# Transformer block on one core: key picking, projections and attention units woven in another order

## The reference, cut to what matters

```python
p = rms_norm(x, mix_norm[l]) @ w_in[l]
pa, pb, pc = split_cols(p, GROUP_SPLITS)
ya = dsa_attention(pa, ...)     # 8 heads; each query sees at most 128 picked keys
yb, v_first = rwkv7_time_mix(pb, ...)   # recurrence, 4 heads
yc = gated_deltanet(pc, ...)            # recurrence, 4 heads
x = x + concatenate([ya, yb, yc], -1) @ w_out[l]

# dsa_attention, for each block i of 128 queries:
score = einsum(relu(logits of 8 index heads), wib)      # 128 queries x 512 keys
_, idx = lax.top_k(score, 128)                          # n_sel = min(256, 512 // 4)
p = softmax(q . k over the picked keys);  o = p @ v
```

## Time and profile before

| | us |
|---|---|
| median of 3 runs (4070.52 to 4078.71) | 4076.85 |
| profiled execution | 4068.68 |
| its span | 4066.7 |
| PE busy | 3803.9 (94%) |
| DVE busy | 1396.7 (34%) |
| ACT busy | 1407.5 (35%) |
| POOL busy | 1339.4 (33%) |
| granted TensorE clock, mean | 0.931 |

### The profile page before, as it was taken

One profiled execution on the slowest core, in us unless ns is written; L12 is line 12 of the kernel. 1 busy time (PEld: TensorE's weight loads), 2 busy tenths in 40 slices (PEclk: granted clock), 3 DMA queues, 4 the chain that ended last, 5 costly groups with the idle time before them and its releaser, 6 DMA issues.

```text
span 4066.7 us, 54295 instructions
## 1 busy us (share of the span) xinstructions
PE 3803.9 (94%) x23012; PEld 3130.1 (77%) x23012; DVE 1396.7 (34%) x2950; ACT 1407.5 (35%) x2395; POOL 1339.4 (33%) x639
## 2 busy tenths in 40 slices
PE   8987999998799979999989789999999999879999
PEld 7876888887588868888757678888888866768887
DVE  2345111334521132113774741112112574662111
ACT  2453222335422233223543432223223454433222
POOL 3103444420244444444210124444444420104443
PEclk9988999998799989999976889999999995889999
DMA  4101333320133333333200023333333310003332
GB/s 118 47 16 58 93 99 96 89 63 11 47 88 98 97 92 100 100 95 95 58 20 2 2 64 98 104 96 102 96 102 93 83 52 1 2 23 88 93 99 93
DMA packets 406785, 292.37 MB, mean 72 GB/s; under 512 B 18032, under 2 KB 356880, under 8 KB 406544
## 3 DMA queue, kind: packets, MB, share of 16 engines
q1 hardware_dynamic: 400976, 284.69, 23.6%
q10 hardware_dynamic: 5136, 2.96, 0.3%
q0 software_dynamic: 432, 1.25, 0.1%
HBM read 286.77 MB, written 2.10 MB: 71 GB/s over the span
## 4 chain that ended last, share of the span: by engine, by line
PE 54%; DVE 6%; ACT 2%; issue 1%; POOL 0%; ACTq 0%; DVEq 0%
PE ps L705 9%; PE ps L706 9%; PE ps L707 9%; PE ps L766 6%; PE ps L769 6%; PE ps L768 6%; PE ps L1285 2%; PE ps L820 2%; PE ps L837 1%; PE ps L1074 1%; PE ps L828 1%; PE ps L688 1%; PE ps L1245 0%; POOL wl L2861 0%; ACT wh L2291 0%
## 5 line engine op out<-in xcount | busy, mean ns | idle before, releaser
L2861 POOL TENSOR_TENSOR wl<-wraw,wh 128x1024 fp32r<-128x1024 f32 (+2 forms) x532 | 1246.3, 2343 | 2258.5 <-ACT wh L2291 2258.5
L705 PE MATMUL ps<-x_T,wh 128*128 128x512 f32 (+1 forms) x2672 | 1028.2, 385 | 18.9 <-POOL wl L2861 9.8
L706 PE MATMUL ps<-x_T,wh 128*128 128x512 f32 (+1 forms) x2672 | 1021.1, 382 | 0.0
L707 PE MATMUL ps<-x_T,wl 128*128 128x512 f32 (+1 forms) x2672 | 1020.7, 382 | 0.0
L2291 ACT ACTIVATE wh<-wraw 128x1024 fp32r<-128x1024 f32 (+2 forms) x532 | 548.8, 1032 | 1104.0 <-PE ps L769 595.0
L705 PEld LDWEIGHTS ps<-x_T,wh 128*128 128x128 f32 x2672 | 510.4, 191 | 130.9 <-issue 30.0
L707 PEld LDWEIGHTS ps<-x_T,wl 128*128 128x128 f32 x2672 | 510.1, 191 | 95.6
L706 PEld LDWEIGHTS ps<-x_T,wh 128*128 128x128 f32 x2672 | 510.5, 191 | 93.5 <-issue 0.5
L766 PE MATMUL ps<-wh,h_T 128*128 128x512 f32 x1056 | 411.3, 390 | 0.0
L769 PE MATMUL ps<-wh,h_T 128*128 128x512 f32 x1056 | 410.9, 389 | 0.0
L768 PE MATMUL ps<-wl,h_T 128*128 128x512 f32 x1056 | 410.8, 389 | 0.0
(11 more groups left out here) (716 smaller groups left out, 4861.4 us busy)
## 6 DMA issues: line engine op xcount, KB each, us to landing
wraw<-in_ffn_w_gate_dram SPq DMA_DIRECT2D x88, 512.0 KB, 3.8
wraw<-in_ffn_w_up_dram SPq DMA_DIRECT2D x88, 512.0 KB, 3.8
wraw<-in_w_in_dram SPq DMA_DIRECT2D x82, 512.0 KB, 3.8
wraw<-in_ffn_w_down_dram SPq DMA_DIRECT2D x80, 512.0 KB, 3.7
wraw<-in_w_gate_dram SPq DMA_DIRECT2D x44, 512.0 KB, 3.8
wraw<-in_w_up_dram SPq DMA_DIRECT2D x44, 512.0 KB, 3.8
wraw<-in_w_down_dram SPq DMA_DIRECT2D x40, 512.0 KB, 3.7
wraw<-in_w_o_dram SPq DMA_DIRECT2D x16, 512.0 KB, 3.7
```

Source lines behind the costliest of these rows:

```text
L705: mm(b[:, t0:t1], wh[:, k, :], xTh[:, k, t0:t1], k == 0, False)
L706: mm(b[:, t0:t1], wh[:, k, :], xTl[:, k, t0:t1], False, False)
L707: ins = mm(b[:, t0:t1], wl[:, k, :], xTh[:, k, t0:t1], False, k == 7)
L2861: tt(wl, raw_of(w), wh.bitcast(F32), ALU.subtract).then_inc(*g.sig("w", "lo", w))
```

## The change

The order of blocks in picking, in their index sums and in the attention units becomes 3, 2, 1 (after block 0 for the units), as `PICKS`. One picking step is made in every round. A column projection's 24 matmuls are split into three pieces of 9, 9 and 6, one in each round (three in a warm-up round), and its bank is held from its first piece to the second piece of the next projection. Its evacuation comes in the round after its last piece. While units of block 3 and 2 are open, units start in even rounds only, and in every round for block 1. `gates` advances in every third round while projections last.

Counted out, the numbered rounds after are: block 0's units start in n = 0, 2, ..., 14; block 3's in n = 18, 20, ..., 32; block 2's in 36, 38, ..., 50; block 1's in every round from 52 to 59. Picking runs for block 3 in n = 1 to 16, block 2 in 18 to 33, block 1 in 35 to 50. Pieces run in n = 0 to 26, the last evacuation in n = 27. The recurrence starts in n = 32, the last unit's last step is in n = 62, and tile 0 has its 32nd step, the last of its solving, in n = 63.

```diff
@@ -291,19 +291,23 @@
         yield
 
 
+PICKS = (3, 2, 1)
+SUMS = [(i, h) for i in PICKS for h in range(8)]
+
+
 def index_lane(skew, summed, work):
 
     for t in range(26):
         if 0 <= t - skew < 24:
-            work(1 + (t - skew) // 8, (t - skew) % 8)
+            work(*SUMS[t - skew])
         if t in (9, 17, 25):
-            summed.add(1 + (t - 9) // 8)
+            summed.add(PICKS[(t - 9) // 8])
         yield
 
 
 def top_lane(summed, masks, first, work, last):
 
-    for i in (1, 2, 3):
+    for i in PICKS:
         while i not in summed:
             yield
         first(i)
@@ -318,11 +322,14 @@
 COLS2 = (6, 0, 1) + tuple(range(7, 13)) + (2, 3, 4, 5)
 
 
-def project_lane(skew, work):
-
-    for t in range(14):
-        if 0 <= t - skew < 13:
-            work(COLS2[t - skew])
+def project_lane(piece, work):
+
+
+    for t in range(40):
+        if t % 3 == 0 and t:
+            work(COLS2[t // 3 - 1])
+        if t < 39:
+            piece(COLS2[t // 3], t % 3)
         yield
 
 
@@ -330,13 +337,15 @@
 
 
 
+
     while next(heads, "end") != "end":
-        next(project)
+        for _ in range(3):
+            next(project)
         next(gates)
         for _ in range(2):
             next(index)
     masks.add(0)
-    todo = [(h, i) for i in range(4) for h in range(8)]
+    todo = [(h, i) for i in (0,) + PICKS for h in range(8)]
     live, n, clear = [], 0, []
     chain = tile_rounds(tiles, clear)
     while todo or live or top:
@@ -349,17 +358,16 @@
         for g in list(live):
             if next(g, "end") == "end":
                 live.remove(g)
-        if todo and (n % 2 == 0 or not project) and todo[0][1] in masks:
+        if todo and (n % 2 == 0 or todo[0][1] == PICKS[-1]) and todo[0][1] in masks:
             live.append(unit(*todo.pop(0)))
             next(live[-1])
         next(index, None)
-        for _ in range(2 if project else 1):
-            if top and next(top, "end") == "end":
-                top = None
-        if project and n % 2 == 0:
+        if top and next(top, "end") == "end":
+            top = None
+        if project:
             if next(project, "end") == "end":
                 project = None
-            else:
+            elif n % 3 == 0:
                 next(gates)
         n += 1
     over()
@@ -584,7 +592,7 @@
         for h in range(4):
             UNITS1 += [("stick", h, 0)] + [("mla", h, i) for i in range(4)]
         UNITS1 += [("swa", h, i) for h in range(4) for i in range(4)]
-        UNITS3 = [("dsa", h, i) for i in range(4) for h in range(8)]
+        UNITS3 = [("dsa", h, i) for i in (0,) + PICKS for h in range(8)]
         GROUP = {"fox": 0, "mla": 1, "stick": 2, "swa": 3}
 
         place = {}
@@ -715,6 +723,29 @@
                     pe.wait_ge(*at(*ready))
                 pe.wait_ge(*at("w", "lo", w))
                 cols_F(w, b, 0, T).then_inc(*pe.sig("w", "used", w))
+
+            def piece_F(_, n):
+
+                if n == 0:
+                    w = use()
+                    _, free = bank(("F", w), ("ev", w), hold=True)
+                    pe.wait_ge(*free)
+                    pe.wait_ge(*at("w", "lo", w))
+                w = wat[0] - 1
+                i = book.bank[("F", w)]
+                if n == 1:
+                    held.discard(book.bank.get(("F", w - 1)))
+                wh, wl = hl_of(w)
+                for k in ((0, 1, 2), (3, 4, 5), (6, 7))[n]:
+                    mm(psum[i][:, :], wh[:, k, :], xTh[:, k, :], k == 0, False)
+                    mm(psum[i][:, :], wh[:, k, :], xTl[:, k, :], False, False)
+                    ins = mm(psum[i][:, :], wl[:, k, :], xTh[:, k, :], False, k == 7)
+                if n == 2:
+                    ins.then_inc(*pe.sig("w", "used", w))
+
+            def last_F(k):
+                if k == COLS2[-1]:
+                    held.discard(book.bank[("F", wat[0] - 1)])
 
             def first_F(name, src, ready, done=()):
 
@@ -1426,7 +1457,7 @@
                 mixer_rounds(heads(l), lambda h, i: unit3(l, ("dsa", h, i)),
                              index_lane(0, summed, lambda i, h: index_sum(l, i, h)),
                              top_lane(summed, masks, nothing, nothing, nothing),
-                             project_lane(0, lambda k: proj_F()), gates(l),
+                             project_lane(piece_F, last_F), gates(l),
                              [rec_tile(l, j, stock) for j in range(4)], masks, over)
                 barrier("o", l)
                 to_T(("out", l), mx, lambda j, c: ("bar", "o", l, "dve"))
@@ -1891,7 +1922,7 @@
 
             def index_sum(l, i, h):
                 acc = msk[:, i - 1, 0:(i + 1) * P]
-                rb = scr[5 + (8 * i + h) % 3]
+                rb = scr[5 + SUMS.index((i, h)) % 3]
                 v.wait_ge(*at("pk", "relu", l, i, h))
                 if h == 0:
                     ins = ts(acc, rb[:, 0:(i + 1) * P], wiv[:, i, h:h + 1], None, ALU.mult)
@@ -2234,7 +2265,7 @@
                 mixer_rounds(heads(l), lambda h, i: unit3(l, ("dsa", h, i)),
                              index_lane(2, summed, partial(index_sum, l)),
                              top_lane(summed, masks, partial(top_first, l), partial(top_step, l), partial(top_last, l)),
-                             project_lane(1, partial(project, l)), rests(16),
+                             project_lane(nothing, partial(project, l)), rests(16),
                              [rec_tile(l, j, stock) for j in range(4)], masks, over)
                 barrier("o", l)
                 for j in range(NT):
@@ -2552,9 +2583,9 @@
                 layer_norm(l, 1)
 
             def index_sum(l, i, h):
-                n = 8 * i + h
-                if n > 10:
-                    s.wait_ge(*at("pk", "acc", l, (n - 3) // 8, (n - 3) % 8))
+                n = SUMS.index((i, h))
+                if n > 2:
+                    s.wait_ge(*at("pk", "acc", l, *SUMS[n - 3]))
                 s.wait_ge(*at("pk", "ix", l, i, h))
                 act(scr[5 + n % 3][:, 0:(i + 1) * P], psum_of("ix", l, i, h)[:, 0:(i + 1) * P],
                     ACT.Relu).then_inc(*s.sig("pk", "relu", l, i, h))
@@ -2822,7 +2853,7 @@
                 mixer_rounds(heads(l), lambda h, i: unit3(l, ("dsa", h, i)),
                              index_lane(1, summed, partial(index_sum, l)),
                              top_lane(summed, masks, nothing, nothing, nothing),
-                             project_lane(1, partial(project, l)), gates(l),
+                             project_lane(nothing, partial(project, l)), gates(l),
                              [rec_tile(l, j, stock) for j in range(4)], masks, over)
                 barrier("o", l)
                 for j in range(NT):
@@ -2998,7 +3029,7 @@
 
                 mixer_rounds(rests(4), lambda h, i: rests(4), index_lane(0, summed, nothing),
                              top_lane(summed, masks, nothing, nothing, nothing),
-                             project_lane(1, lambda k: use()), rests(16),
+                             project_lane(nothing, lambda k: use()), rests(16),
                              [rec_tile(l, j, stock) for j in range(4)], masks, over)
                 barrier("o", l)
                 use(4)
```

## The result

The changed kernel takes 4017.48 us (median of 4 runs, 4015.34 to 4021.24) beside 4077.78 for the kernel before in the same comparison: ratio 0.9859 with an interval of 0.9844 to 0.9873, or 60 us less. The forecast was 4058, with a range of 4030 to 4100. The profiled execution took 4015.34, its span 4013.4 instead of 4066.7, with a mean granted clock of 0.945 instead of 0.931.

The account below looks back on a forecast made before the run. PE was taken as the bound, for long stretches at half its clock. Terms of +3.5 - 4.2 + 0.8 - 3.6 - 6 = -9.5 us a layer, -19 for both, took 4076.85 to 4058 us, range 4030 to 4100.

Parts of the forecast that it names:

- Start: Per layer, up to the first score of n = 0: warm-up index +3.5 us, shorter wait for DVE -4.2.
- Rounds 0 to 27: Rounds with projections, per layer: 85.8 us against 85.0 before, so +0.8, with DVE hidden.
- The index term: Index matmuls in rounds 0 to 27, two of them at 1.06 us and sixteen shorter: 13.5 us.
- Rounds 28 to 62: Rounds after the projections, per layer: 114.9 us against 118.5 before, -3.6, from cold work, waits and clock.
- Waits +9: In n = 32 to 51, PE waits for DVE or ACT add 9 us a layer, bounds 0 and 30.
- The middle's clock: In n = 28 to 47 the clock would be near 0.5.
- rival 4: PE keeps its clock through half of n = 28 to 47: another -10 us a layer, 4038 us, chance 14%.
- The tail, -12: n = 48 to 62: solving steps bring the clock back, 43 us for 15 rounds instead of 55, so -12.
- After over(): From `over()` to tile 1 made: solved tile 0 takes 5.3 us off DVE, the bound there, -6 us a layer.
- Rival 1: The tail (n = 48 to 62) stays cold, without the -12: 4082 us, chance 24%.
- Rival 2: In n = 32 to 51 the chain's waits set rounds, 23 us more per layer: 4104 us, chance 17%.
- Rival 3: The clock falls in the first rounds with pieces of nine matmuls: +42 us a layer, 4142 us, chance 5%.

Follow-up runs that it names:

- Experiment 3: Changed kernel with two picking steps a round again while the projections last: 4057.94 us, 0.9956 to the kernel before.
- Experiment 2: Changed kernel with all 24 matmuls of a projection run whole in every third round, bank still held: 4092.73 us, 1.004 to the kernel before.
- experiment 1: Changed kernel with the blocks in the order 1, 2, 3 again, all else kept: 4065.39 us, 0.9973 to the kernel before.
- experiment 6: Kernel before plus three useless matmuls of 512 columns in each of rounds n = 20 to 43: 4046.8 us, 0.9931 to the kernel before.
- experiment 7: Changed kernel plus three useless matmuls of 512 columns in each of rounds n = 28 to 47: 4010.31 us, 0.9848 to the kernel before.
- experiment 8: Changed kernel with tile 0 stopped at 16 steps, no solving step before `over()`: 4031.16 us, 0.9893 to the kernel before.
- Experiment 4: Changed kernel with tile 0 limited to 22 steps before `over()`, the rest done beside making tile 1: 4005.32 us, 0.9826 to the kernel before.

## Why the prediction was right, and where it was wrong

**Start: held.** Its sum was -0.7 and it is -2.2. The warm-up's last transposes start 3.3 us later (1985.88 against 1982.55), as the forecast of +3.5 had it; the wait went from 5.76 to 0.25, not to 1.6, and 1.15 came back before the first index matmul.

**Rounds 0 to 27: held, with a cover I had not priced.** 85.8 forecast, 86.1 measured, clock 1.00 in both layers, and PE idle for 1.6 us in all of them. That it agrees to 0.3 is partly luck. The index term, 13.5, counts two groups of 512 columns that do not exist: all eight of block 3 run in the warm-up, and the sixteen left take 0.84 and 0.63 us, 11.8 together. The idle time of 1.6 us, of which the sum had nothing, makes up for most of that. Experiment 3 confirms that DVE was near: with two steps a round it is the bound. But I counted splitting as 18 starts of a group. Experiment 2 shows what it does beside that: it fills the rounds in which a unit is on its way over DVE and ACT.

**Rounds 28 to 62: the step that failed**, by 20.7 of 114.9 us. It failed in three terms.
- *Waits +9.* The forecast had 7 us of idle PE from before and 9 more, 16 in all, by the rate of one stretch of the earlier trace rows. Measured were 58.0 - 51.6 = 6.4 in the middle: -9.6. All five waits there are for units' exponentials and copies (ACT L2636 and L2641), none stands at a matmul of the chain, and the last is before 2109. The rate of the earlier trace rows came from rounds with a picking step of block 3 and units of block 1 and 2; it did not carry over to rounds with units of block 3 and 2. That these cover more is likely, but no run tests it.
- *The middle's clock.* "n = 28 to 47 clock near 0.5" is wrong: 0.63 and 0.73. By subtraction (114.9 less 43 for the tail and 16 of waits leaves 55.9 of cold work) it is 51.6 us instead, -4.3. This is rival 4 at less than half of its price of 10.
- *The tail, -12.* The clock did come back, but only at about 2143 us, at the end of the third of its fifteen rounds. I took 2.9 us a round from a loop of waits; there was none (PE is idle for 0.3 us in the whole tail), and the rounds went at PE's pace: 36.3 us from 2132.06 to 2168.38 instead of 43, -6.7.

These are -20.6 together, all but 0.1 of the miss. That the clock decides what the tail costs is shown (experiments 1, 6, 7 and 8). What brings it back, in the middle and in the tail, is not: experiments 3 and 7 have tails of the same make that stay cold.

**After over(): the mechanism held, the size did not.** DVE has 24.4 - 19.3 = 5.1 us less, for a forecast of 5.3. But the stretch got only 2.8 shorter, for a forecast of 6. The waits between 2170 and 2197 (engine, line, what it waited for: us in total, times, longest) show why:

```profile
PE ps L1202 <- DVE arena L2069: 3.1, 1, 3.1
...
PE ps L1316 <- DVE spare L2161: 2.8, 1, 2.8
...
PE ps L1231 <- DVE scr L2105: 1.7, 1, 1.7
...
PE ps L1239 <- DVE arena L2113: 1.6, 1, 1.6
```

These are 9.2 of 27 us in four waits, each for the step before it in the recurrence: what bounds there is the chain of dependent steps, not DVE's sum. PE also lost its clock behind the first of them: its two groups on L1202 and L1204 take 2.04 and 1.91 us, where the kernel before, which had solving steps to run in that wait, needed 1.10 and 1.02 (stretch clock 0.75 against 0.92). How much of the missing 3.2 us is that was not separated. Experiment 4 uses this: the solving put back costs 3 us after `over()` and saves 7 before.

**The rivals.** Rival 1 (tail cold) did not happen here, but is what the change becomes in layer 1 with the old order (76 us at 0.50). Rival 2 (waits take over) is refuted by PE's 6.4 us of idle time in the middle. Rival 3 (clock falls in the first rounds) did not happen: 1.00 with pieces of nine and one bank fewer. The Trainium skill's rule for it (TensorE: Matmul & The Clock Gate, "A second HAM failure mode: psum-queue depth-cycling") would have lost the clock, since it sees small idle times between groups that cycle through banks. This case's trace does not show them (PE is busy 28.00 of 28 us at 1.00 from 2046 on), and it was the long groups of experiment 2, with 0.79, that lost it, behind waits for exponentials. Rival 4 came in part.

**The parts do not add up.** Undoing the order costs 48 us, the splitting 75, the single picking step 40: 163 for a change worth 60. Whatever else it does, each undone part costs PE its clock somewhere: 0.79 in front without the splitting, 0.50 and 0.55 in a tail without the order and with two picking steps.

## What to carry to other kernels

A stretch in which PE is always busy is not at its limit while its granted clock is at half: read clock and busy share together, and ask which order or which neighbours would bring the clock back before counting matmuls. Spread long dense groups over the rounds as cover for short dependent steps, and give light dependent work (here the last solving levels) to a stretch in which another chain waits anyway. A rate of waits read from one mix of work should not be carried to another without asking what covers each of them.

## What the runs showed of the hardware that was not expected

- The kernel before became 28 us faster with 144 useless matmuls of 512 columns (three in 24 rounds of two layers, 0.96 us a round at the full clock). The fully busy tail was at 0.51 without them and at 1.00 with them.
- PE busy 75.1 of 76 us, with 593 matmuls, stayed at 0.50 (experiment 1, layer 1); in the change 550 matmuls, with the lighter units of blocks 2 and 1 between the same solving steps, took 38 us at 0.86.
- With identical code, one execution had a tail at 1.00 in one layer and at 0.53 in the other, 23 us apart (34 and 57, experiment 7), and the runs of that kernel lie within 20 us rather than the 6 us of the change.
